# First block's output projection in rounded parts and rests, with its weights split during the attention

## The chip, the cores and the metric

The kernel runs on one core of one Trainium2 chip. The metric is the device time of one execution in microseconds (us), as the median of several runs; lower is better. The engines are TensorE (PE in the profile, with its weight loads as PEld), VectorE (DVE), ScalarE (ACT), GpSimd (POOL) and SyncE (SP), which issues the weight transfers. Each engine works through its own queue in order and waits on semaphores that other engines raise.

## The reference, cut to what matters

Two transformer blocks of two layers each run one after the other. Only the first block is touched. Each of its layers mixes tokens by two kinds of attention and a pooling, and projects the joined result back to the model width of 1024:

```python
def token_mix(qg, kg, vg, qm, km, vm, pool_in, w_pool, ls_pool, w_out):
    og = attention(qg, kg, vg, HEAD_DIM ** -0.5)       # 6 heads of 64
    om = attention(qm, km, vm, MLA_QK ** -0.5)         # 6 heads of 64
    op = multiscale_pool(pool_in, w_pool, ls_pool)     # 256 columns
    return jnp.concatenate([merge_heads(og), merge_heads(om), op], axis=-1) @ w_out
...
x_lat = x_lat + gt1 * mix
x_lat = x_lat + gt2 * sq_relu_mlp(modulate(rms_norm(x_lat, g_norm2[i]), sh2, sc2), w_mlp1[i], w_mlp2[i])
```

`w_out` is 1024 x 1024 for each layer. Layer 0 does this for 512 tokens (256 context and 256 latent tokens), layer 1 for the 256 latent tokens only. All data is float32.

## The kernel before, in words

Activations lie transposed: 128 features on the partitions, tokens along the free dimension, in 8 chunks `k` of 128 features. The mixed output is `mixT`, which is the same memory as `hT`. Its chunks 0 to 2 come from the first kind of attention, 3 to 5 from the second, 6 and 7 from the pooling. Weights come through a ring of three slots of 2 MB (`ring`), each 1024 rows by 512 columns, loaded by SP in the order of `plan_slots`; a slot is refilled when `slot_release` says that its last reader is done.

There are two ways of multiplying. The plain one uses float32 operands as they are (one instruction in the program, two matmul records in the trace). The split one cuts each operand into a part rounded to the format fp32r and the rest, also fp32r, and adds three products: high x high, high x low, low x high. MLP and second block work so. Their weights are split in **granules** of 128 output columns (8 chunks x 128 columns): ACT writes the rounded part with one copy of 128x1024 (`hi_to`, L1615), DVE the rest with one subtraction (`lo_to`, L2059), and PE's `split_product` (L1160 to L1173) waits for `lo_ready` and issues 24 matmuls. In the first block's MLP granules go through two buffers (`MLP_BUFS`), and a third one at its start. `split_by(key)` says up to which granule ACT and DVE are to split once the product `key` is done.

**Attention** (loops at L1295, L1709 and L2158). A step `j` takes 128 queries of a pair of heads: PE makes scores (L1309), DVE takes the maximum (L2165), ACT the exponential with its sum (L1736), DVE scales by the reciprocal (L2175, L2176) one step later, PE transposes the weights (L1327) two steps later, ACT copies them out of PSUM (L1726), and every second step PE multiplies by the values (L1341, bank key `"o"`) and DVE copies the result into `mixT` (L2199, L2201). Layer 0 has 24 steps, in which PE also computes modulation rows; layer 1 has 12. Two last steps compute the pooling products (L1351), which DVE copies with a gain (L2188).

**Output projection** (L1355 to L1371). It is a plain product: 8 products `m` of 128 output features, 8 chunks each, in the order 6, 7, 0 to 5. In layer 0, three small transposes of parameters (L1106) lie between the first products. As each product ends, DVE adds it with its gate to `xT` (`residual`, L2140), ACT squares the new `xT` chunk (`square_summed`, L1575) and POOL adds up the squares (L911); PE sums them over partitions (L1056, L1058), ACT takes logarithm and exponential (L1585 to L1587), DVE does one Newton step (L2042, L2044), and DVE, ACT and DVE again make the normed, shifted, rounded input of the MLP (L2083, L1625, L2068), whose first products (L1185 to L1187) follow it chunk by chunk.

The first three granules of the MLP are split by ACT after its square of chunk 2, and by DVE after its residual 5.

Of the kernel before, what the change touches and what calls it, by code (L numbers as in the profile page):

```python
# [15 lines left out]
P = 128  # L16
# [293 lines left out]

WOUT_ORDER = (6, 7, 0, 1, 2, 3, 4, 5)

# [25 lines left out]
def granules_of(i):  # L338

    g = []  # L340
    for name, _, n in mlp_slots(i):
        for m in range(4):
            key = (("a", i), "up", 4 * n + m) if name == "up" else (("a", i), "down", n % BLOCKS, n // BLOCKS * 4 + m)
            g.append(((name, i, n), m, key))
    return g


# [57 lines left out]
def program(nc, A, out):  # L405
# [5 lines left out]
    with ExitStack() as ctx:  # L411
# [65 lines left out]
        big_r = rounded_view("big", [P, 16384])  # L477
        h_hi, h_lo = hT_r, big_r[:, 2 * KC * TOK:3 * KC * TOK].rearrange("p (k t) -> p k t", k=KC)
        hid_hi, hid_lo = (big_r[:, j * KC * TOK:(j + 1) * KC * TOK].rearrange("p (k t) -> p k t", k=KC) for j in range(2))
        gran = big_r[:, 3 * KC * TOK:].rearrange("p (b a k c) -> p b a k c", b=2, a=2, k=KC)  # L480
# [60 lines left out]
        buffers = {("mlp", "third"): pair(over(3)), ("b", "h"): (hT_r[:, :, SEQ:SEQ + P], hT_r[:, :, SEQ + P:TOK]), ("b", "end"): pair(over(7)),  # L541
                   ("b", "spare"): spare, ("b", "norms"): norms, ("b", "mqk"): pair(over(4))}
        for r in range(MLP_BUFS):
            buffers["mlp", r] = (gran[:, r, 0], gran[:, r, 1])
# [35 lines left out]
        roped = sem("roped")  # L580
        pooled = sem("pooled")
        padded = sem("padded")
        nmax_ready = sem("nmax_ready")
# [109 lines left out]

        for i in range(DEPTH):
            phase(("mlp", i), granules_of(i), lambda j: ("mlp", "third" if j == 2 else (j + (j > 2)) % MLP_BUFS))
        for l in range(DEPTH):
# [30 lines left out]
        def split_by(key):  # L727

            n = gran_of[key]
            if key[0][0] == "a":  # L730
                return min(n + 1 + MLP_BUFS + (key[1] == "up" and key[2] < 2), gran_cap[n])
            return min(n + 1 + B_BUFS, gran_cap[n])
# [279 lines left out]
        def _(pe):  # L1012
# [147 lines left out]

            def split_product(n, hi, lo, T):
# [6 lines left out]
                for k in range(KC):  # L1168
                    await_chunk(k)
                    mm(b[:, 0:T], w_hi[:, k, :], hi(k), start=(k == 0), stop=False)  # L1170
                    mm(b[:, 0:T], w_hi[:, k, :], lo(k), start=False, stop=False)  # L1171
                    last = mm(b[:, 0:T], w_lo[:, k, :], hi(k), start=False, stop=(k == KC - 1))  # L1172
                fill(last, key)  # L1173
# [27 lines left out]
            for i in range(DEPTH):  # L1201
# [152 lines left out]

                for n in range(2):  # L1355
                    w = slot(("wout", i, n))
                    for m in range(4):
                        key = (tag, "wout", 4 * n + m)
                        b = start_bank(key)
                        for k in WOUT_ORDER:  # L1360
                            if n == m == 0 and k in (6, 7):
                                await_drained(pe, (tag, "pool", k - 6))
                            if n == m == 0 and k == 0:
                                await_drained(pe, (tag, "o", len(groups) - len(sets) - 1))
                            if n == m == 0 and k == 5:
                                await_drained(pe, (tag, "o", len(groups) - 1))
                            last = mm(b[:, 0:TOK - t0], w[:, k, m * P:(m + 1) * P], mixT[:, k, t0:TOK],  # L1367
                                      start=(k == WOUT_ORDER[0]), stop=(k == WOUT_ORDER[-1]))
                        fill(last, key)
                        if i == n == 0 and m > 0:  # L1370
                            params_transposed(m)  # L1371
                summed_squares((tag, "n2"), TOK - t0)
# [4 lines left out]
                for j, (name, _, _) in enumerate(mlp_slots(i)):  # L1377
                    for m in range(4):
                        n = first_gran["mlp", i] + 4 * j + m
                        if (j, m) == (0, 0):  # L1380
                            split_products_in_step(n, lambda k: h_hi[:, k, t0:TOK], lambda k: h_lo[:, k, t0:TOK], TOK - t0)
                        elif (j, m) == (0, 1):
                            if i == 0:
                                mod_column(MOD_NORM)
                        elif name == "up":
                            split_product(n, lambda k: h_hi[:, k, t0:TOK], lambda k: h_lo[:, k, t0:TOK], TOK - t0)
                        else:
                            if (4 * j + m) % 16 == 8:

                                source[0] = (up_ready, n // 16 * KC, 1)  # L1390
                            split_product(n, lambda k: hid_hi[:, k, t0:TOK], lambda k: hid_lo[:, k, t0:TOK], TOK - t0)
# [158 lines left out]
        def _(act):  # L1550
# [138 lines left out]
            for i in range(DEPTH):  # L1689
# [24 lines left out]
                steps = 2 * len(groups)  # L1714
                base = sum(24 * len(sets_of(j)) for j in range(i))
                await_drained(act, (tag, f"km{MH - 1}", 0))
                for j in range(steps + 2):
# [199 lines left out]
        def _(dve):  # L1917
# [225 lines left out]

            nm = [0]
            for i in range(DEPTH):
# [13 lines left out]
                for j in range(steps + 3):  # L2159
# [31 lines left out]
                    if 0 <= g < len(groups) and not odd:  # L2191
# [259 lines left out]
```

## Time and profile before

| what | value |
|---|---|
| median of 3 runs | 1812.45 us (1810.99 to 1812.68) |
| the profiled execution | 1810.93 us, span 1809.1 us |
| PE busy | 1747.5 us, 97% of the span |
| DVE, ACT, POOL busy | 61%, 50%, 25% |
| output projection, layer 0 | 249.7 to 305.8 us |
| output projection, layer 1 | 822.0 to 849.9 us |
| split matmuls, all lines | more than half of the chain of waits |

The span is counted from the first to the last instruction of the profiled execution; the device time also holds what lies around it. Busy shares say how long an engine had an instruction in work, not that it was at its peak.

### The profile page before, as it was taken

Reading aid. Unit: us, or ns where it says so; the run is one execution under the profiler, and the core shown is the slowest. Engines: PE = TensorE matmul, PEld = TensorE weight load, DVE = VectorE, ACT = ScalarE, POOL = GpSimd, SP = SyncE. Lnnn points to the kernel's source line nnn. Section 1 sums busy time; section 2 is a strip of 40 time slices with the busy share of each in tenths; the row PEclk is TensorE's granted clock in tenths of the full one; section 3 lists DMA queues with packets and bytes.
Section 4 is the critical chain, followed back from the end, with each engine's and each line's share of the span. In section 5 each row is a group of like instructions: output and inputs, shape, how many; then the busy total and the mean of one; then the engine's idle time right before and its main releaser. Section 6 shows DMA issues by size and latency. Waiting matters only on the chain.

```text
span 1809.1 us, 28680 instructions
## 1 busy us (share of the span) xinstructions
PE 1747.5 (97%) x10708; PEld 1424.0 (79%) x10708; DVE 1104.5 (61%) x1975; ACT 901.4 (50%) x1936; POOL 460.6 (25%) x864
## 2 busy tenths in 40 slices
PE   6999998999999998988999989999999899999998
PEld 3453553888888885647999989899899898998998
DVE  4228743887878433583555577676556686685555
ACT  3237622535353523563555566576554565674542
POOL 1017001000000010331000025057771161287730
PEclk9999999999999998999999999999999999999999
DMA  9323313455555321202445533533335335433351
GB/s 345 131 93 136 136 56 126 154 186 187 186 187 186 139 74 47 94 1 94 151 176 185 187 140 107 205 121 141 140 141 187 140 106 186 143 139 132 121 193 45
DMA packets 127540, 255.26 MB, mean 141 GB/s; under 512 B 2462, under 2 KB 7212, under 8 KB 127404
## 3 DMA queue, kind: packets, MB, share of 16 engines
q1 hardware_dynamic: 126406, 251.16, 38.8%
q0 software_dynamic: 704, 2.10, 0.4%
q8 instruction: 87, 1.43, 0.3%
q14 instruction: 49, 0.40, 0.1%
q10 hardware_dynamic: 294, 0.18, 0.0%
HBM read 252.38 MB, written 1.05 MB: 140 GB/s over the span
## 4 chain that ended last, share of the span: by engine, by line
PE 92%; DVE 4%; ACT 2%; issue 1%; DMA 0%; POOL 0%; SPq 0%; DVEq 0%; ACTq 0%
PE ps L1170 19%; PE ps L1172 18%; PE ps L1171 18%; PE ps L1195 6%; PE ps L1367 5%; PE ps L1309 2%; PE ps L1044 2%; PE ps L1428 2%; PE ps L1426 2%; PE ps L1427 2%; PE ps L1341 2%; PE ps L1327 1%; PE ps L1117 1%; PE ps L1071 1%; PE ps L1506 1%; PE ps L1509 1%
## 5 line engine op out<-in xcount | busy, mean ns | idle before, releaser
L1615 ACT ACTIVATE big_r<-ring 128x1024 fp32r<-128x1024 f32 x198 | 209.1, 1058 | 370.3 <-PE ps L1172 342.2
L2059 DVE TENSOR_TENSOR big_r<-ring,big_r 128x1024 fp32r<-128x1024 f32 x198 | 245.7, 1242 | 219.0 <-ACT big_r L1615 219.0
L1171 PE MATMUL ps<-big_r 128*128 128x256 f32 (+1 forms) x1088 | 360.6, 331 | 0.0
L1170 PE MATMUL ps<-hT_r,big_r 128*128 128x256 f32 (+1 forms) x848 | 270.6, 319 | 0.0
L1172 PE MATMUL ps<-hT_r,big_r 128*128 128x256 f32 (+1 forms) x848 | 265.6, 313 | 0.0
L911 POOL TENSOR_TENSOR sq<-sq 128x256 f32<-128x256 f32 (+1 forms) x30 | 37.1, 1238 | 741.7 <-ACT sq L1575 741.4
L1171 PEld LDWEIGHTS ps<-big_r 128*128 128x128 f32 x1088 | 206.8, 190 | 18.6
L1170 PE MATMUL ps<-big_r 128*128 128x256 f32 (+1 forms) x592 | 196.3, 332 | 1.4 <-DVE big_r L2226 1.4
L1172 PE MATMUL ps<-big_r 128*128 128x256 f32 (+1 forms) x592 | 194.8, 329 | 0.0
L1172 PEld LDWEIGHTS ps<-hT_r,big_r 128*128 128x128 f32 x848 | 161.5, 190 | 9.6
L1170 PEld LDWEIGHTS ps<-hT_r,big_r 128*128 128x128 f32 x848 | 161.6, 191 | 9.1
L2059 DVE TENSOR_TENSOR cst_r<-ring,w_ukv_sb_r 128x1024 fp32r<-128x1024 f32 x70 | 87.5, 1251 | 57.0 <-ACT w_ukv_sb_r L1615 56.9
L1170 PEld LDWEIGHTS ps<-big_r 128*128 128x128 f32 x592 | 112.5, 190 | 12.0 <-DVE big_r L2226 2.2
L1615 ACT ACTIVATE w_ukv_sb_r<-ring 128x1024 fp32r<-128x1024 f32 x70 | 74.0, 1058 | 95.6 <-PE ps L1172 83.5
L1172 PEld LDWEIGHTS ps<-big_r 128*128 128x128 f32 x592 | 112.5, 190 | 10.2
L2025 DVE SCALAR_TENSOR_TENSOR pT<-ring,csilu,pT 128x512 f32<-128x512 f32 x168 | 118.5, 747 | 1.3
L1195 PE MATMUL ps<-hT,ring 128*128 128x512 f32 (+1 forms) x288 | 107.4, 530 | 10.0 <-ACT hT L1636 9.9
L1170 PE MATMUL ps<-hT_r,w_ukv_sb_r 128*128 128x256 f32 x384 | 111.8, 291 | 0.0
L2042 DVE SCALAR_TENSOR_TENSOR nt<-ps,nt 128x256 f32<-128x256 f32 (+3 forms) x74 | 38.9, 526 | 114.9 <-ACT nt L1587 114.4
L1172 PE MATMUL ps<-hT_r,cst_r 128*128 128x256 f32 x384 | 108.2, 282 | 0.0
L1171 PE MATMUL ps<-xT_r,w_ukv_sb_r 128*128 128x256 f32 x384 | 107.7, 281 | 0.0
L1195 PEld LDWEIGHTS ps<-hT,ring 128*128 128x128 f32 x288 | 56.2, 198 | 58.9 <-issue 51.7
(317 smaller groups left out, 4332.0 us busy)
## 6 DMA issues: line engine op xcount, KB each, us to landing
ring<-in_w_in SPq DMA_DIRECT2D x44, 2048.0 KB, 7.8
ring<-in_w_mlp SPq DMA_DIRECT2D x32, 2048.0 KB, 7.7
ring<-in_w_mod SPq DMA_DIRECT2D x24, 2048.0 KB, 8.0
ring<-in_w_out SPq DMA_DIRECT2D x4, 2048.0 KB, 7.6
ring<-in_w_out_a SPq DMA_DIRECT2D x4, 2048.0 KB, 7.8
ring<-in_w_out_b SPq DMA_DIRECT2D x4, 2048.0 KB, 7.9
ring<-in_w_o SPq DMA_DIRECT2D x4, 2048.0 KB, 7.6
ring<-in_w_in SPq DMA_DIRECT2D x2, 1152.0 KB, 10.1
```

Source lines behind the costliest of these rows:

```text
L911: nc.gpsimd.tensor_tensor(sum_slot(0, T), sum_slot(0, T), sum_slot(k, T), ALU.add).then_inc(sq_summed, 1)
L1044: last = mm(b[0:parts, 0:T], ones, sq[0:parts, n % SQ, 0:T], start=(j == 0), stop=(j == chunks - 1))
L1170: mm(b[:, 0:T], w_hi[:, k, :], hi(k), start=(k == 0), stop=False)
L1171: mm(b[:, 0:T], w_hi[:, k, :], lo(k), start=False, stop=False)
L1172: last = mm(b[:, 0:T], w_lo[:, k, :], hi(k), start=False, stop=(k == KC - 1))
L1195: last = mm(b[0:cols, 0:T], w[:, k, m:m + cols], src(k), start=(k == 0), stop=(k == KC - 1))
L1309: fill(mm(banks[e][:, 0:tiles * P], lhs, rhs, start=True, stop=True), (tag, "s", 2 * j + e))
L1367: last = mm(b[:, 0:TOK - t0], w[:, k, m * P:(m + 1) * P], mixT[:, k, t0:TOK], start=(k == WOUT_ORDER[0]), stop=(k == WOUT_ORDER[-1]))
L1615: act_fn(hi, raw, ACT.Copy).then_inc(hi_ready, 1)
L2025: ins = V.scalar_tensor_tensor(acc, w, c, acc, ALU.mult, ALU.add)
L2042: drain(V.scalar_tensor_tensor(r2, bank(key)[0:parts, 0:T], width * EPS, r2, ALU.add, ALU.mult), key)
L2059: V.tensor_tensor(lo, raw, hi.bitcast(F32), ALU.subtract).then_inc(lo_ready, 1)
```

## The change

Both output projections become split products. The order of the granules is put ahead of each layer's MLP, 8 granules per layer, in three buffers laid over memory that the attention has finished with (the pooling's work area, keys and values). Granule 0 is split during the attention (ACT in step `steps - 3`, DVE in `steps - 2`), granule 1 at its end, granule 2 behind the mixed output's last chunk, and the other five as products free their buffers (`OUT_SPLIT`). The MLP's first granules are split behind residuals 5, 6 and 7.

The mixed output is split too: ACT copies each chunk rounded into `mix_hi` (over the first heads' queries, keys and values), DVE subtracts it in place. For chunks 0 to 4 this is put into the steps in `MIX_STEPS`; 6, 7 and 5 follow the last step. PE takes the chunks in `MIX_ORDER` and waits for each in the first product.

```diff
-WOUT_ORDER = (6, 7, 0, 1, 2, 3, 4, 5)
+MIX_ORDER = (0, 1, 2, 3, 4, 6, 7, 5)
+MIX_STEPS = ({16: 0, 17: 1, 18: 2, 20: 3, 24: 4}, {9: 0, 10: 1, 11: 2, 12: 3, 13: 4})
+OUT_BUFS = (0, 1, 2, 0, 1, 2, 1, 2)
+OUT_SPLIT = (4, 5, 6, 6, 7, 8, 8, 8)
...
+def granules_out(i):
+    return [(("wout", i, m // 4), m % 4, (("a", i), "wout", m)) for m in range(KC)]
...
         def split_by(key):
             n = gran_of[key]
+            if key[1] == "wout":
+                return first_gran["wout", key[0][1]] + OUT_SPLIT[key[2]]
...
 # PE
-                for n in range(2):
-                    w = slot(("wout", i, n))
-                    for m in range(4):
...
-                            last = mm(b[:, 0:TOK - t0], w[:, k, m * P:(m + 1) * P], mixT[:, k, t0:TOK],
-                                      start=(k == WOUT_ORDER[0]), stop=(k == WOUT_ORDER[-1]))
+                source[0] = (mix_ready, KC * i, 1)
+                for m in range(KC):
+                    split_product(first_gran["wout", i] + m, lambda k: mix_hi[k][:, t0:TOK], lambda k: hT_r[:, k, t0:TOK],
+                                  TOK - t0, MIX_ORDER)
...
 # ACT
+                def mix_rounded(k, made):
+                    await_drained(act, (tag,) + made)
+                    act_fn(mix_hi[k][:, t0:TOK], mixT[:, k, t0:TOK], ACT.Copy).then_inc(mix_hi_ready, 1)
...
+                    if j in MIX_STEPS[i]:
+                        k = MIX_STEPS[i][j]
+                        mix_rounded(k, ("o", made[k]))
+                    if j == steps - 3:
+                        act.wait_ge(pooled, (4, 6)[i])
+                        hi_to(o0 + 1)
+                    if j == steps:
+                        hi_to(o0 + 2)
+                for c in range(2):
+                    mix_rounded(6 + c, ("pool", c))
+                mix_rounded(5, ("o", len(groups) - 1))
+                hi_to(o0 + 3)
                 for k in range(KC):
-                    square_summed((tag, "n2"), k, (tag, "wout", k), t0)
-                    if k == 2:
-                        hi_to(first_gran["mlp", i] + MLP_BUFS + 1)
+                    key = (tag, "wout", k)
+                    await_bank(act, key)
+                    hi_to(split_by(key))
+                    square_summed((tag, "n2"), k, key, t0)
+                    if k in (5, 6):
+                        hi_to(first_gran["mlp", i] + (1 if k == 5 else MLP_BUFS + 1))
...
 # DVE
+                V.tensor_tensor(hT_r[:, k, cols], mixT[:, k, cols], mix_hi[k][:, cols].bitcast(F32), ALU.subtract)\
+                    .then_inc(mix_ready, 1)
...
+                    if j - 1 in MIX_STEPS[i]:
+                        mix_rest()
+                    if j == steps - 2:
+                        lo_to(first_gran["wout", i] + 1)
+                    if j == steps + 1:
+                        lo_to(first_gran["wout", i] + 2)
+                while n_mix[0] < KC * (i + 1):
+                    mix_rest()
...
+                lo_to(first_gran["wout", i] + 3)
                 for m in range(KC):
+                    lo_to(split_by((tag, "wout", m)))
                     residual((tag, "wout", m), m, i, 16, s0)
...
-                    if m == 5:
-                        lo_to(g0 + MLP_BUFS + 1)
+                    if m >= 5:
+                        lo_to(g0 + m - 4)
```

## Rows read from the trace of the kernel before

**Rows 1.** The page: the chain of waits, its share of the span by engine.

```profile
PE 92%; DVE 4%; ACT 2%; issue 1%; DMA 0%; POOL 0%; SPq 0%; DVEq 0%; ACTq 0%
```

**Rows 2.** Windows: stretch, us, busy us (instructions) by engine, clock, DMA share, GB/s.

```profile
249.70:305.80 56.10, 56.10 (x133) 24.74 (x133) 16.22 (x41) 7.13 (x10) 8.39 (x6) 1.00 0.10 38
```

**Rows 3.** Timeline (start us, us, engine, line): the last residual of layer 0's projection.

```profile
305.80 0.88 DVE L2140 SCALAR_TENSOR_TENSOR xT<-ps,mod,xT 128x256 f32<-128x256 f32 x2 [5.99 <-PE ps L1367]
```

**Rows 4.** Timeline, layer 1's projection: PE, a square and a split, last residual.

```profile
821.99 27.89 PE L1367 MATMUL ps<-hT,ring 128*128 128x256 f32 x128
...
833.18 0.42 ACT L1575 ACTIVATE sq<-xT 128x256 f32<-128x256 f32 x1 [3.04 <-DVE xT L2140]
833.50 1.04 ACT L1615 ACTIVATE big_r<-ring 128x1024 fp32r<-128x1024 f32 x1
...
849.93 0.48 DVE L2140 SCALAR_TENSOR_TENSOR xT<-ps,mod,xT 128x256 f32<-128x256 f32 x1 [2.10 <-PE ps L1367]
850.44 0.42 ACT L1575 ACTIVATE sq<-xT 128x256 f32<-128x256 f32 x1 [2.16 <-DVE xT L2140]
```

**Rows 5.** Timeline, MLP: successive products of 512 tokens, then of 256.

```profile
370.54 0.87 DVE L2140 SCALAR_TENSOR_TENSOR xT<-ps,mod,xT 128x256 f32<-128x256 f32 x2
375.99 0.87 DVE L2140 SCALAR_TENSOR_TENSOR xT<-ps,mod,xT 128x256 f32<-128x256 f32 x2
...
905.03 1.06 ACT L1615 ACTIVATE big_r<-ring 128x1024 fp32r<-128x1024 f32 x1 [1.82 <-PE ps L1172]
906.12 1.23 DVE L2059 TENSOR_TENSOR big_r<-ring,big_r 128x1024 fp32r<-128x1024 f32 x1 [1.26 <-ACT big_r L1615]
907.26 0.48 DVE L2140 SCALAR_TENSOR_TENSOR xT<-ps,mod,xT 128x256 f32<-128x256 f32 x1
907.91 1.06 ACT L1615 ACTIVATE big_r<-ring 128x1024 fp32r<-128x1024 f32 x1 [1.82 <-PE ps L1172]
```

**Rows 6.** Timeline, MLP: rounding and rest of 512 tokens, rest of 256.

```profile
329.87 0.63 ACT L1768 ACTIVATE big_r<-sq 128x512 fp32r<-128x512 f32 x1
334.40 0.68 DVE L2226 TENSOR_TENSOR big_r<-sq,big_r 128x512 fp32r<-128x512 f32 x1
...
866.01 0.42 DVE L2226 TENSOR_TENSOR big_r<-sq,big_r 128x256 fp32r<-128x256 f32 x1
```

**Rows 7.** Timeline, end of layer 0's attention, idle time before in brackets.

```profile
240.43 0.69 DVE L2165 TENSOR_REDUCE stat<-ps 128x1 f32<-128x512 f32 x1 [0.62 <-PE ps L1309]
...
242.72 1.22 PE L1327 MATMUL ps<-cst,pb 128*128 128x128 f32 x8 [0.24 <-DVE pb L2176]
...
246.55 0.60 ACT L1726 ACTIVATE rstd<-ps 128x512 f32<-128x512 f32 x1 [1.97 <-PE ps L1327]
```

**Rows 8.** Timeline, end of layer 1's attention.

```profile
812.34 0.69 DVE L2165 TENSOR_REDUCE stat<-ps 128x1 f32<-128x512 f32 x1 [0.62 <-PE ps L1309]
...
813.97 1.09 ACT L1726 ACTIVATE pT<-ps 128x512 f32<-128x512 f32 x2 [2.52 <-PE ps L1327]
...
814.62 1.22 PE L1327 MATMUL ps<-cst,pb 128*128 128x128 f32 x8 [0.59 <-ACT pT L1726]
```

**Rows 9.** Timeline, layer 1: splits of DVE beside sums of POOL.

```profile
843.42 4.01 DVE L2059 TENSOR_TENSOR big_r<-ring,big_r 128x1024 fp32r<-128x1024 f32 x3
...
844.03 1.19 POOL L911 TENSOR_TENSOR sq<-sq 128x256 f32<-128x256 f32 x1 [2.73 <-ACT sq L1575]
...
848.36 0.72 POOL L911 TENSOR_TENSOR sq<-sq 128x256 f32<-128x256 f32 x1 [3.14 <-ACT sq L1575]
```

**Rows 10.** The window behind layer 1's projection, and two matmuls in it.

```profile
855.00:861.00 6.00, 5.28 (x25) 5.31 (x26) 5.70 (x13) 3.28 (x8) 0.00 (x0) 0.51 0.34 123
...
855.72 0.55 PE L1185 MATMUL ps<-hT_r,big_r 128*128 128x256 f32 x1 [4.11 <-DVE big_r L2068]
...
856.29 0.41 PE L1187 MATMUL ps<-hT_r,big_r 128*128 128x256 f32 x1
856.50 0.41 PE L1185 MATMUL ps<-hT_r,big_r 128*128 128x256 f32 x1
```

More of the change, by code:

```diff
@@ L478, in program @@
         h_hi, h_lo = hT_r, big_r[:, 2 * KC * TOK:3 * KC * TOK].rearrange("p (k t) -> p k t", k=KC)
+        mix_hi = [big_r[:, o:o + TOK] for o in [k * TOK for k in range(5)] + [4608 + k * TOK for k in range(3)]]
         hid_hi, hid_lo = (big_r[:, j * KC * TOK:(j + 1) * KC * TOK].rearrange("p (k t) -> p k t", k=KC) for j in range(2))
@@ L542, in program @@
                    ("b", "spare"): spare, ("b", "norms"): norms, ("b", "mqk"): pair(over(4))}
+        for r, o in enumerate((13376, 8192, 10240)):
+            v = big_r[:, o:o + 2 * KC * P].rearrange("p (a k c) -> p a k c", a=2, k=KC)
+            buffers["out", r] = (v[:, 0], v[:, 1])
         for r in range(MLP_BUFS):
@@ L581, in program @@
         pooled = sem("pooled")
+        mix_hi_ready = sem("mix_hi_ready")
+        mix_ready = sem("mix_ready")
         padded = sem("padded")
@@ L694, in program @@
         for i in range(DEPTH):
+            phase(("wout", i), granules_out(i), lambda j: ("out", OUT_BUFS[j]))
             phase(("mlp", i), granules_of(i), lambda j: ("mlp", "third" if j == 2 else (j + (j > 2)) % MLP_BUFS))
@@ L1159, in await_chunk, with split_product @@
                         source[0] = None
-            def split_product(n, hi, lo, T):
+            def split_product(n, hi, lo, T, order=tuple(range(KC))):
                 key = granules[n][2]
@@ L1167, in split_product @@
                 w_hi, w_lo = gran_bufs[n]
-                for k in range(KC):
-                    await_chunk(k)
-                    mm(b[:, 0:T], w_hi[:, k, :], hi(k), start=(k == 0), stop=False)
+                for j, k in enumerate(order):
+                    await_chunk(j)
+                    mm(b[:, 0:T], w_hi[:, k, :], hi(k), start=(j == 0), stop=False)
                     mm(b[:, 0:T], w_hi[:, k, :], lo(k), start=False, stop=False)
-                    last = mm(b[:, 0:T], w_lo[:, k, :], hi(k), start=False, stop=(k == KC - 1))
+                    last = mm(b[:, 0:T], w_lo[:, k, :], hi(k), start=False, stop=(j == KC - 1))
                 fill(last, key)
@@ L1353, in _ @@
                         fill(last, key)
-                for n in range(2):
-                    w = slot(("wout", i, n))
-                    for m in range(4):
[L1358 to L1366, printed above, removed]
-                            last = mm(b[:, 0:TOK - t0], w[:, k, m * P:(m + 1) * P], mixT[:, k, t0:TOK],
-                                      start=(k == WOUT_ORDER[0]), stop=(k == WOUT_ORDER[-1]))
-                        fill(last, key)
-                        if i == n == 0 and m > 0:
-                            params_transposed(m)
+                source[0] = (mix_ready, KC * i, 1)
+                for m in range(KC):
+                    split_product(first_gran["wout", i] + m, lambda k: mix_hi[k][:, t0:TOK], lambda k: hT_r[:, k, t0:TOK],
+                                  TOK - t0, MIX_ORDER)
+                    if i == 0 and 0 < m < 4:
+                        params_transposed(m)
                 summed_squares((tag, "n2"), TOK - t0)
@@ L1388, in _ @@
                             if (4 * j + m) % 16 == 8:
-                                source[0] = (up_ready, n // 16 * KC, 1)
+                                source[0] = (up_ready, (i * BLOCKS + j // 4) * KC, 1)
                             split_product(n, lambda k: hid_hi[:, k, t0:TOK], lambda k: hid_lo[:, k, t0:TOK], TOK - t0)
@@ L1715, in _ @@
                 base = sum(24 * len(sets_of(j)) for j in range(i))
+                o0 = first_gran["wout", i]
+                def mix_rounded(k, made):
+                    await_drained(act, (tag,) + made)
+                    act_fn(mix_hi[k][:, t0:TOK], mixT[:, k, t0:TOK], ACT.Copy).then_inc(mix_hi_ready, 1)
+                half, n_sets = len(groups) // 2, len(sets)
+                made = [half - 1] * 3 + [half + n_sets - 1, half + 2 * n_sets - 1]
                 await_drained(act, (tag, f"km{MH - 1}", 0))
@@ L2142, in residual, with mix_rest @@
                 drain(last, key)
-            nm = [0]
+            n_mix = [0]
+            def mix_rest():
+                i, k = n_mix[0] // KC, MIX_ORDER[n_mix[0] % KC]
+                n_mix[0] += 1
+                dve.wait_ge(mix_hi_ready, n_mix[0])
+                cols = slice(t0_of(i), TOK)
+                V.tensor_tensor(hT_r[:, k, cols], mixT[:, k, cols], mix_hi[k][:, cols].bitcast(F32), ALU.subtract)\
+                    .then_inc(mix_ready, 1)
             for i in range(DEPTH):
```

## Prediction

> **What bounds the kernel now.** I read the chain of waits first: PE has 92% of it [rows 1], so the time is the sum of PE's work and the few places where PE waits. The window of layer 0's projection then shows PE busy in 56.10 of 56.10 us at full clock, DVE in 16.2, ACT in 7.1, DMA at 0.10 [rows 2]: this stage costs what its matmuls cost, and both engines that the change loads have room. The timelines give its ends: from the window's start to the last residual at 305.80 in layer 0, 56.1 us [rows 2, 3]; 821.99 to 849.93 in layer 1, 27.9 us [rows 4]. Last come the ends of the attentions, where small work is put between steps: DVE sat idle only 0.62 us before a maximum, and PE already waits there, 0.24 us for DVE in layer 0 and 0.59 us for ACT in layer 1 [rows 7, 8].
>
> **Part 1, PE in layer 0.** Removed: 8 plain products in 56.1 us, of which three small transposes take about 0.6, so 6.94 each. Added: 8 split products of 24 matmuls at 512 tokens. The MLP makes exactly these; two residuals behind successive ones start 5.45 us apart [rows 5]. 8 x 5.45 + 0.6 = 44.2. Gain 11.9 us, if PE is fed.
>
> Is it fed? A granule after product m costs in a row: ACT's rounding, then DVE's rest 1.09 later, DVE's residual 1.14 behind that [rows 5] and lasting 0.88, ACT's square about 0.65 (as the 0.63 rounding of the same width [rows 6]). That is 3.8 us against 5.45 for a product, and each granule is wanted two products after its buffer is free (one product later for the last two). The parameters' copies and scalings come behind products 1 to 3 on DVE, whose 16.2 us with them leave room for 8 rests of 1.23 in 44 [rows 2]. At the end: product 5 ends at t; split of granule 7, residual and square to t+3.8; first MLP granule's rest done at t+6.2; residual 6 to t+7.1, square to t+7.8, next rounding and rest to t+10.1. Product 7 ends at t+10.9 and finds DVE free. Nothing lost in layer 0.
>
> **Part 2, PE in layer 1.** The same products at 256 tokens take 2.88 us (granule roundings at 905.03 and 907.91 [rows 5]), 8 x 2.88 = 23.0 instead of 27.9. By PE alone 4.9 less. But here the row of ACT and DVE is longer than the product. ACT's square to its next rounding 0.32 (833.18 to 833.50 [rows 4]), rounding to rest 1.09, rest to residual 1.14 [rows 5], residual to square 0.51 (849.93 to 850.44 [rows 4]): 3.06 us per link, and the order of the code forces it: ACT rounds granule n+1 only behind its square n, which waits for residual n, which DVE does only behind rest n. With S the start of product 0: product 4 ends at S+14.4, by when product 3, which splits nothing, has let the engines catch up. Then rounding of granule 6, its rest and residual 4 at S+14.4+0.05+1.09+1.14 = S+16.7. Three links follow (granule 7 with residual 5, MLP granule 0 with residual 6, MLP granule 1 with residual 7): residual 7 at S+16.7+9.2 = S+25.9, though its product is done at S+23.0. Granule 6 is ready at S+16.7 and wanted at S+17.3, granule 7 at S+19.8 and wanted at S+20.2, so PE itself waits little; only the tail is late. Against S+27.9 before [rows 4] the gain is 2.0, not 4.9.
>
> **Part 3, work put into the attentions.** Per layer DVE gets 5 rests of chunks and 2 of granules, ACT 5 roundings of chunks and 2 of granules, before the last step ends. In layer 0 a chunk is 0.63 on ACT and 0.68 on DVE [rows 6], a granule 1.06 and 1.23. ACT waited 1.97 us for PE before its copies of the last step [rows 7], longer than chunk 4 or granule 1 alone, and somewhat like it in the steps before; it takes them in. DVE does too with single chunks. The rest of granule 0 however (step 22) lies before a maximum with 0.62 us of idle time, and PE's transposes behind it already waited 0.24 for DVE [rows 7]: 1.23 - 0.62 = 0.6 us on the path. Bounds: 0, and everything on DVE, 5 x 0.68 + 2 x 1.23 = 5.9. I take 0.6, by the nearest row.
>
> In layer 1 step 10 has a chunk (0.42 [rows 6]) and granule 0 together, 1.65 us before a maximum with 0.62 idle, so 1.0 later on DVE; PE's transposes begin at 814.62 and end 1.2 us later, a part of the delay falls on their second half, and what reaches the values' product I put at 0.8. ACT's own 1.5 us in step 9 vanish in 2.52 us of waiting two steps on [rows 8]. Bounds 0 and 5 x 0.42 + 2 x 1.23 = 4.6; I take 0.8.
>
> **Part 4, the new wait of product 0.** It waits chunk by chunk for `mix_ready`. Behind it on PE are all further products, on the others nothing before the first residual. The last attention result is copied by DVE (0.42), then in layer 1 four rests (chunks 4, 6, 7, 5) of 0.42 on DVE, with ACT's rounding of 5 (0.42, as its square of this width [rows 4]) beside them: ready 2.2 us after PE's last value product. PE comes to chunk 5, the eighth, after 7/8 of 2.88 = 2.5. In layer 0 it is 0.42 + 3 x 0.68 = 2.5 against 4.8. Price 0; if the cover goes, as much as DVE is late, at most some 1.5 us (granule 1's rest plus a handover) in layer 1.
>
> **Part 5, behind the projection.** After residual 7 one more MLP rest (1.23) is on DVE. Beside it run ACT's square and three functions of 0.42 each before DVE is wanted, 1.7 us without PE's sums: hidden. Slots are released earlier, when granules 3 and 7 are split; DMA has nothing to do there (share 0.10 [rows 2]). PE idles longer in layer 1, from S+23.0. Behind the idle 4.11 us the clock was granted at 0.51 in 855 to 861, matmuls 0.21 us apart [rows 10] instead of 2.88/24 = 0.12: that is the 1.2 GHz level. After the change the fall may come before the last sum of squares; two float32 records of 256 tokens more slowly, 0.3 us. Bounds -1 (it rises sooner) and +2.
>
> What DVE and POOL do to each other speaks against the change. Three rests took 4.01 us instead of 3.7, and the POOL sum beside them 1.19 instead of 0.72 [rows 9]. In the new order a sum of 256 tokens runs during ACT's rounding (1.09 until DVE starts) and is out of the way, so I put nothing into the sum. The Trainium skill, GPSIMD Engine Reference, Specifications, says that GpSimd shares its SBUF interfaces with VectorE, with contention against instructions that have two SBUF inputs, as the rests do. The trace agrees by those numbers. By that rule alone each of six rests in layer 1 that met a sum would be 0.1 us longer, 0.6 us in all.
>
> **Sum.** Layer 0: -11.9 + 0.6. Layer 1: -2.0 + 0.8. Behind: +0.3. Together -12.2 us. The profiled execution took 1810.93 (span 1809.1, 1.8 outside it) and would take 1798.7. It lies 1.5 us below the median 1812.45; I apply the difference to the median: 1800.2.
>
> **Rivals.**
> - *Layer 1 follows PE.* If ACT and DVE run ahead of the order above, residual 7 comes at S+23.0: 2.9 more, -15.1, 1797.3. For it: DVE was busy in 16.2 of 56.1 us of such a stage [rows 2]. Against: the links are fixed by the queues' order. 0.12.
> - *The attentions pay for all of it.* DVE's added work comes fully onto the path, 5.9 + 4.6 instead of 1.4: +9.1, so -3.1, 1809.3. For: PE waits for DVE and ACT there already. Against: ACT's idle times of 1.97 and 2.52 us [rows 7, 8]. Halfway, 1804.8, is likelier than the whole. Together 0.13, of which the full case 0.07.
> - *Granules come late.* PE in layer 1 is held by each link, 8 x 3.06, and in layer 0 by the buffers, one link of 3.8 us lost: -8, 1804. Against: buffers are three. 0.07.
> - *Slower: the clock falls in the projection.* The waits for chunks in product 0 and the late tail let it fall to the lower level and stay there. At 0.21 us per matmul of 256 tokens [rows 10] and twice that at 512, a product takes 5.1 and 10.3 us. 8 x (10.3 - 5.45) + 8 x (5.1 - 2.88) = 57 us more than in the forecast, so 1857. It decides once about a fifth of the matmuls (12.2 of 57) run so. Against: it stood at 1.00 through the whole plain stage [rows 2], and the MLP's split products kept their pace at full clock [rows 5]. 0.03.
> - *It does not do what it says*: a wait of granule 0 for pooling or weights moves the splitting behind the attention; each layer then starts some 3 us late, 1806. Against: the slots were asked for long before, DMA was at 0.10 when the stage began [rows 2]. 0.03.
>
> **How the numbers follow.** The forecast has 0.62, with 1797.5 to 1803 as its own range. With the others, 8 in 10 lie within 1796.5 to 1805.5. Within 0.2% of 1812.45, about what can be told from no change, is 1808.8 to 1816.1: the full attention case, 0.07. Slower 0.03, faster 0.90.
>
> **What would show it.** The new profile should have split matmuls 0.227 us apart in layer 0 and a stage of 44 to 45 us; in layer 1, residual 7 about 26 us after the stage begins with PE idle nearly 3 us before it, and residuals in its last third 3.1 us apart, not 2.9. The values' product of the last group should come 0.6 and 0.8 us later after the attention's start. I am wrong if layer 1's stage takes 23 us, if PE waits over 1 us inside product 0, or if the first projection starts over 2 us late.

## The result, and the profile after

The changed kernel takes 1797.98 us, the median of 5 runs (1795.74 to 1801.34), beside 1810.99 for the kernel before in the same rounds: a ratio of 0.993, with an interval of 0.9913 to 0.9948. It is 13.0 us faster (9 to 16); 1800.2 and -12.2 were forecast. The profiled execution is the one of 1797.98, so its trace can stand for the median.

The page of the changed kernel, its first part:

```profile
span 1796.1 us, 29026 instructions
PE 1731.1 (96%) x10836; PEld 1433.7 (80%) x10836; DVE 1127.6 (63%) x2007; ACT 924.6 (51%) x1968; POOL 459.8 (26%) x864
```

DVE and ACT have each gained some 23 us of work, PE has lost 16, and the span is 13.0 us shorter: it went with PE, not with the helpers. Windows of the changed kernel, with the columns of [rows 2]: layer 0's projection, then layer 1's tail:

```profile
250.10:295.00 44.90, 44.90 (x198) 36.51 (x197) 22.77 (x49) 14.43 (x18) 7.74 (x6) 1.00 0.26 94
833.00:843.00 10.00, 3.44 (x17) 2.14 (x16) 6.10 (x9) 4.57 (x10) 0.73 (x1) 0.72 0.54 202
```

The first row answers to [rows 2]: PE is again busy in all of it at full clock, the stage is just shorter. The second shows where layer 1 is not PE's. Timeline of the changed kernel, layer 0: the end of the attention, the first split matmuls, the last residual:

```profile
240.08 1.22 DVE L2091 TENSOR_TENSOR big_r<-ring,big_r 128x1024 fp32r<-128x1024 f32 x1
241.21 1.28 DVE L2206 TENSOR_REDUCE stat<-ps 128x1 f32<-128x512 f32 x2
243.23 1.22 PE L1346 MATMUL ps<-cst,pb 128*128 128x128 f32 x8 [0.40 <-DVE pb L2217]
...
250.17 0.50 PE L1189 MATMUL ps<-big_r 128*128 128x512 f32 x1
...
254.17 0.39 PE L1191 MATMUL ps<-big_r 128*128 128x512 f32 x1
254.40 0.39 PE L1189 MATMUL ps<-big_r 128*128 128x512 f32 x1
254.62 0.39 PE L1190 MATMUL ps<-hT_r,big_r 128*128 128x512 f32 x1
...
295.02 0.88 DVE L2172 SCALAR_TENSOR_TENSOR xT<-ps,mod,xT 128x256 f32<-128x256 f32 x2 [0.62 <-PE ps L1191]
```

The rest of granule 0 now stands before the maximum, and PE's wait for DVE behind it is 0.40 us where it was 0.24 [rows 7]. The matmuls start 0.23 us apart. From the first of them to the last residual it is 44.85 us; it was 56.1 [rows 2, 3].

Timeline of the changed kernel, layer 1: a wait in the attention, and the last three links of the row of ACT and DVE, with PE's sums of squares:

```profile
803.78 1.22 PE L1346 MATMUL ps<-cst,pb 128*128 128x128 f32 x8 [1.08 <-DVE pb L2217]
...
831.21 0.48 DVE L2172 SCALAR_TENSOR_TENSOR xT<-ps,mod,xT 128x256 f32<-128x256 f32 x1
831.72 0.42 ACT L1583 ACTIVATE sq<-xT 128x256 f32<-128x256 f32 x1 [1.69 <-DVE xT L2172]
832.04 1.04 ACT L1623 ACTIVATE big_r<-ring 128x1024 fp32r<-128x1024 f32 x1
833.12 1.23 DVE L2091 TENSOR_TENSOR big_r<-ring,big_r 128x1024 fp32r<-128x1024 f32 x1 [1.44 <-ACT big_r L1623]
834.26 0.48 DVE L2172 SCALAR_TENSOR_TENSOR xT<-ps,mod,xT 128x256 f32<-128x256 f32 x1
...
836.19 0.67 PE L1075 MATMUL ps<-sq,cst 128*128 128x256 f32 x2 [1.65 <-POOL sq L930]
...
837.36 0.48 DVE L2172 SCALAR_TENSOR_TENSOR xT<-ps,mod,xT 128x256 f32<-128x256 f32 x1
...
838.39 1.22 PE L1077 MATMUL ps<-sq,cst 128*128 128x256 f32 x2 [1.53 <-ACT sq L1583]
```

Residuals start at 831.21, 834.26 and 837.36: 3.05 and 3.10 us apart, against the 2.88 of a product. PE is done at about 834.5 and waits 1.65 us, then 1.53 us more. The stage begins at 811.15, so residual 7 comes 26.21 us behind it, where it was 27.94 [rows 4].

| us | before | after | difference | forecast |
|---|---|---|---|---|
| layer 0: first scores to projection | 84.67 | 84.83 | +0.16 | +0.6 |
| layer 0: projection to last residual | 56.14 | 44.85 | -11.3 | -11.9 |
| layer 1: first scores to projection | 45.37 | 45.86 | +0.49 | +0.8 |
| layer 1: projection to last residual | 27.94 | 26.21 | -1.7 | -2.0 |
| layer 1: last residual to first Newton step | 3.12 | 3.69 | +0.57 | +0.3 |
| sum | | | -11.8 | -12.2 |

Of the other 1.2 us, 0.57 lie behind that Newton step: to the first matmul of the MLP's third product, the first that does not go chunk by chunk behind the normed input, it was 10.78 us and is 10.21. The others are pieces of 0.4 to 0.6 us, with either sign, elsewhere in code that is not changed. Between two profiles an untouched stretch can differ by more. Layer 1's attention is the same code in x1_residual_first below, and took 47.32 us there instead of 45.86. A window at its start, in that run, has the reason:

```profile
763.60:766.90 3.30, 3.30 (x8) 1.47 (x10) 0.80 (x3) 0.00 (x0) 3.14 (x5) 0.50 0.00 0
```

The clock was granted at 0.50 there, up to 766.9; in the changed kernel it was 1.00 in this stretch. From the first scores to the first ones of the second kind of attention it is 16.92 us in x1 and 15.46 in the changed kernel, which is the whole difference of 1.46. For the pieces of 0.4 to 0.6 I give no cause.

### The profile page after: what moved, and what is told of

It reads as the page before. It is cut to its first block, busy times and chain, and to the rows that moved or that the text cites. A ratio compares the mean times of both kernels' runs of the same rounds, so it can differ in the third digit from the quotient of the medians.

```text
span 1796.1 us, 29026 instructions
## 1 busy us (share of the span) xinstructions
PE 1731.1 (96%) x10836; PEld 1433.7 (80%) x10836; DVE 1127.6 (63%) x2007; ACT 924.6 (51%) x1968; POOL 459.8 (26%) x864
## 4 chain that ended last, share of the span: by engine, by line
PE 51%; DVE 1%; ACT 1%; issue 0%; POOL 0%; DVEq 0%; ACTq 0%
PE ps L1189 12%; PE ps L1191 12%; PE ps L1190 12%; PE ps L1436 2%; PE ps L1434 2%; PE ps L1435 2%; PE ps L1514 1%; PE ps L1517 1%; PE ps L1509 1%; PE ps L1090 1%; PE ps L1063 1%; PE ps L1480 1%; PE ps L1204 0%; PE ps L1205 0%; ACT big_r L1623 0%; DVE big_r L2091 0%
## 5 line engine op out<-in xcount | busy, mean ns | idle before, releaser
L2091 DVE TENSOR_TENSOR big_r<-ring,big_r 128x1024 fp32r<-128x1024 f32 x214 | 263.9, 1233 | 249.3 <-ACT big_r L1623 249.2
L1623 ACT ACTIVATE big_r<-ring 128x1024 fp32r<-128x1024 f32 x214 | 226.2, 1058 | 370.8 <-PE ps L1191 358.3
L1190 PE MATMUL ps<-big_r 128*128 128x256 f32 (+1 forms) x1088 | 360.6, 331 | 0.0
L1189 PE MATMUL ps<-big_r 128*128 128x256 f32 (+1 forms) x720 | 239.9, 333 | 1.4 <-DVE big_r L2277 1.4
L1191 PE MATMUL ps<-big_r 128*128 128x256 f32 (+1 forms) x720 | 237.9, 330 | 0.0
L1190 PEld LDWEIGHTS ps<-big_r 128*128 128x128 f32 x1088 | 206.8, 190 | 18.7
L1189 PEld LDWEIGHTS ps<-big_r 128*128 128x128 f32 x720 | 136.8, 190 | 15.2 <-DVE big_r L2277 2.2
L1191 PEld LDWEIGHTS ps<-big_r 128*128 128x128 f32 x720 | 136.8, 190 | 12.8
```

Source lines behind the costliest of these rows:

```text
L1189: mm(b[:, 0:T], w_hi[:, k, :], hi(k), start=(j == 0), stop=False)
L1623: act_fn(hi, raw, ACT.Copy).then_inc(hi_ready, 1)
L2091: V.tensor_tensor(lo, raw, hi.bitcast(F32), ALU.subtract).then_inc(lo_ready, 1)
```

## The experiments

My theory was that of the forecast: layer 0 follows PE; layer 1 follows the order rounding, rest, residual, square; granule 0's rest is the price in the attentions; the chunks cost nothing. The rival in layer 1 was that PE or contention bounds it, and in the attentions that each added split has its share of the price. Effects under 1 us are read from stages in the profiles, since times of one kernel spread over 2 to 6 us. All edits are to the changed kernel.

**x1_residual_first.** DVE does the residual ahead of the next rest.

```diff
 for m in range(KC):
-    lo_to(split_by((tag, "wout", m)))
     residual((tag, "wout", m), m, i, 16, s0)
+    lo_to(split_by((tag, "wout", m)))
```

> On VectorE each residual of the projection goes ahead of the rest of the next granule instead of behind it; all else is the changed kernel. Theory (layer 1's stage is set by the order rounding, rest, residual, square, 3.06 us a link): with the residual first a granule is ready 2.3 us after its buffer is free and the square does not wait for it, so links vanish among the projection's own granules; the MLP's granules still stand before residuals 6 and 7. Residual 7 of layer 1 starts 24.2 us after the stage begins instead of 26.2, layer 0 unchanged (44.9 us). Rival (the order is harmless, PE or the clock holds layer 1): 26.2 stays.

Measured: 1796.77 (one run; before 1810.64). Layer 1's stage is 24.67 us (811.90 to 836.57), layer 0's 44.86 as before the edit. The same instructions in another order give 1.5 us: it is the order, not DVE's load. The last three residuals still have a rest between them that only the MLP wants. The stage is 0.5 us longer than expected, and 0.4 of that is one rest. Timeline of this kernel, layer 1, DVE and POOL:

```profile
830.64 2.90 DVE L2091 TENSOR_TENSOR big_r<-ring,big_r 128x1024 fp32r<-128x1024 f32 x2 [0.69 <-ACT big_r L1623]
831.00 1.47 POOL L930 TENSOR_TENSOR sq<-sq 128x256 f32<-128x256 f32 x1 [1.41 <-ACT sq L1583]
...
833.47 0.47 DVE L2172 SCALAR_TENSOR_TENSOR xT<-ps,mod,xT 128x256 f32<-128x256 f32 x1
```

The second of the two rests started beside the sum and took 1.65 us instead of 1.23, and residual 6 came right behind it.

**x2_tail_free.** As x1, and the rests of the first MLP granules moved behind their residuals:

```diff
-                    if m >= 5:
-                        lo_to(g0 + m - 4)
+                    if m == KC - 2:
+                        lo_to(g0 + 1)
+                lo_to(g0 + MLP_BUFS + 1)
```

> As the kernel before it, and also the rests of the MLP's first granules are moved on VectorE: the first behind residual 6, the other two behind residual 7. Theory: residual 7 of layer 1 starts when its product is done, 23.1 us after the stage begins (26.2 in the changed kernel), so 3.0 us less in all; two rests of 1.23 us fit ahead of the Newton step. Layer 0 unchanged. The clock may fall later too: 0 to 0.6 us more. Rival (the Newton step becomes late because two rests lie before it): 1 us is given back. Total 1795 if the theory holds, 1798 if not.

Measured: 1793.47 (1792.75 to 1794.96, 4 runs; ratio to before 0.9913, 0.9897 to 0.993). Timeline of this kernel, layer 1, DVE, and PE's first matmul of the stage:

```profile
809.32 0.39 PE L1189 MATMUL ps<-big_r 128*128 128x256 f32 x1
...
826.90 0.49 DVE L2172 SCALAR_TENSOR_TENSOR xT<-ps,mod,xT 128x256 f32<-128x256 f32 x1 [0.48 <-PE ps L1191]
828.07 1.23 DVE L2091 TENSOR_TENSOR big_r<-ring,big_r 128x1024 fp32r<-128x1024 f32 x1 [0.69 <-ACT big_r L1623]
829.78 0.48 DVE L2172 SCALAR_TENSOR_TENSOR xT<-ps,mod,xT 128x256 f32<-128x256 f32 x1 [0.48 <-PE ps L1191]
830.18 1.21 DVE L2091 TENSOR_TENSOR big_r<-ring,big_r 128x1024 fp32r<-128x1024 f32 x1
832.65 0.48 DVE L2172 SCALAR_TENSOR_TENSOR xT<-ps,mod,xT 128x256 f32<-128x256 f32 x1 [1.26 <-PE ps L1191]
```

Each residual now waits for PE, in brackets, where in the changed kernel it came straight behind a rest. They are 2.88 and 2.87 us apart, and the stage is 23.33 us: 8 x 2.88 and the last residual's handover. Now layer 1 follows PE, and the 2.9 us between the forecast and its first rival are what the order had cost in this stage. (In time the medians differ by 4.5 us; 0.5 more lie between residual 7 and the Newton step, see part 5 below, and the rest is within what the times spread.)

**x3_granule0_later.** Granule 0's rest goes behind the last step's maximum and scaling, in both layers (`j == steps - 2` becomes `j == steps`).

> On VectorE the rest of projection granule 0 goes from step steps-2 to step steps, where no maximum follows. Theory (granule 0 ahead of a maximum costs 0.5 us in each attention): PE waits no more 0.4 us in layer 0 and 1.1 us in layer 1 for the scaled weights, and both projections begin about 0.5 us earlier in their attentions. Rival (single chunks cost it, or another wait stands right behind): the starts do not move.

Measured: 1796.55 (one run). Timeline of this kernel in layer 0:

```profile
240.31 0.69 DVE L2206 TENSOR_REDUCE stat<-ps 128x1 f32<-128x512 f32 x1 [0.62 <-PE ps L1328]
...
242.60 1.22 PE L1346 MATMUL ps<-cst,pb 128*128 128x128 f32 x8 [0.24 <-DVE pb L2217]
...
245.29 1.22 DVE L2091 TENSOR_TENSOR big_r<-ring,big_r 128x1024 fp32r<-128x1024 f32 x1
```

The idle 0.62 before the maximum and PE's wait of 0.24 are those of [rows 7] again, with the rest behind them. Layer 1's attention takes 45.37, the number of before. The other profiles bear this out: from the first scores of the second kind to the projection, layer 1 takes 30.40 or 30.41 us wherever this rest stands ahead of the maximum (the changed kernel, x1, x2, x4, x6, x10) and 29.91 where it does not (before, x3, x7, x8, x9); in layer 0 it is likewise 48.93 or 48.94 with it and 48.77 or 48.78 without. So all of the price was this rest, and the other splits had none, but in layer 0 it was 0.16 us and not the 0.5 that I expected here too.

**x5_no_spread.** The five first chunks are split behind the attention and not in its steps: `MIX_STEPS = ({}, {})`, and ACT rounds chunks 0 to 4 ahead of the pooled ones.

> The changed kernel with no chunk of the mixed output split inside the attention: chunks 0 to 4 are rounded and subtracted behind the last step, ahead of 6, 7 and 5. Theory (single chunks inside the steps cost nothing, so taking them out wins nothing; what they save is a wait in product 0): the way from the ninth attention result to the last one is as in the changed kernel, and product 0 waits for its first chunk (copy 0.4, rounding 0.3 to 0.6, rest 0.4 to 0.7 us) and then nearly keeps pace, so 1 to 2 us more in each layer before product 0 ends. Rival (the chunks in the steps are what delays the attentions): the projections start earlier by 0.2 and 0.5 us.

Measured: 1798.85 (one run). From layer 0's copy of the sixth last group (the first of the second kind) to that of the last it takes 31.86 us, with the chunks inside the steps 31.87: in there they were free. Timeline of this kernel at the start of the projections, DVE's last copy, its rests, and PE's first split matmul in layers 0 and 1:

```profile
250.96 0.42 DVE L2244 COPY hT<-ps 128x256 f32<-128x256 f32 x1 [1.17 <-PE ps L1360]
251.30 3.09 DVE L2185 TENSOR_TENSOR hT_r<-hT,big_r 128x512 fp32r<-128x512 f32 x5
...
252.13 0.47 PE L1189 MATMUL ps<-big_r 128*128 128x512 f32 x1 [1.21 <-DVE hT_r L2185]
...
812.70 0.35 PE L1189 MATMUL ps<-big_r 128*128 128x256 f32 x1 [0.94 <-DVE hT_r L2185]
```

Product 0 waits 1.21 us for chunk 0 and then keeps its pace, as the chunks come faster than PE's three matmuls each. From the last copy's start to residual 7 it is 45.96 us instead of 44.74 in layer 0, 27.08 instead of 26.10 in layer 1. So spreading them is worth 1.2 and 1.0 us.

**x9_layer0_only, x6_layer1_only.** The change in one layer, the plain projection of before with its granules' slots in the other; each product, granule split and chunk split is put under `if i == ONLY`.

> The split projection in layer 0 alone, the plain one in layer 1. Theory (the gains of the layers add, nearly all is layer 0's): stage of layer 0 44.9 us, of layer 1 27.9 us; 11 us less than before, 1799.5 by a median of 1810.7. Rival (part of the gain comes only with both): under 9 less.

> The split projection in layer 1 alone; layer 0 has the plain one of the kernel before. Theory (layer 1 wins 1.7 in its stage and pays 0.5 before it, 0 to 0.6 us of clock behind it): 1.2 us less than before, 1809.5 by a median of 1810.6; stage of layer 0 56.1 us, of layer 1 26.2 us. Rival (layer 1 follows PE): 4.4 less.

Measured: layer 0 alone 1798.35 (1798.16 to 1801.21, 4 runs; before 1810.77; ratio 0.9936, 0.9919 to 0.9953), its stage 44.84 us and the plain one of layer 1 27.93. Layer 1 alone 1809.82 (1807.77 to 1811.47, 10 runs; before 1810.73; ratio 0.9996, 0.9987 to 1.0006), its stage 26.23. The layers add up: -12.4 and -0.9 beside -13.0. Layer 1's part can't be told from nothing in time; only its profile shows it: 1.7 gained in the stage and 0.5 paid back ahead of it. The 0.57 us that the changed kernel paid behind it are not there: from the last residual to the Newton step it is 3.17 us, against 3.12 before.

**x4_two_terms.** The products of the projections leave out the matmul of the weights' rests, so the output is less exact; PE has 16 of 24 matmuls, ACT and DVE all their work.

```diff
-                    last = mm(b[:, 0:T], w_lo[:, k, :], hi(k), ...)
+                    if not two:
+                        last = mm(b[:, 0:T], w_lo[:, k, :], hi(k), ...)
```

> The projection leaves out its third term, the rest of the weights times the rounded mixed output; the rests are still made. 16 instead of 24 matmuls per product. Theory: layer 0 is PE's, 5.45 us a product, and becomes 3.63 us by PE, then is held by the link of ScalarE and VectorE at 512 tokens, about 3.7 us plus the parameters' work: residual 7 at about 33 instead of 44.9 us after the stage begins. Layer 1 is the engines' order already: 26.2 becomes 25.5 to 26.2 though a third of its matmuls is gone. Rival (PE holds both): layer 1 becomes 15.4 us + tail, under 21.

Measured: 1784.75 (one run). Timeline of this kernel, residuals of layer 1, whose first split matmul starts at 800.91:

```profile
815.43 0.47 DVE L2173 SCALAR_TENSOR_TENSOR xT<-ps,mod,xT 128x256 f32<-128x256 f32 x1
818.48 0.48 DVE L2173 SCALAR_TENSOR_TENSOR xT<-ps,mod,xT 128x256 f32<-128x256 f32 x1
821.53 0.48 DVE L2173 SCALAR_TENSOR_TENSOR xT<-ps,mod,xT 128x256 f32<-128x256 f32 x1
824.63 0.48 DVE L2173 SCALAR_TENSOR_TENSOR xT<-ps,mod,xT 128x256 f32<-128x256 f32 x1
```

And PE's first matmul of product 5:

```profile
812.03 0.36 PE L1189 MATMUL ps<-big_r 128*128 128x256 f32 x1 [0.91 <-DVE big_r L2092]
```

With a third of PE's work gone they are still 3.05, 3.05 and 3.10 us apart: the link of 3.06 sets the pace, not PE. The stage is 23.72, though, and I had expected 25.5 to 26.2. That was my error: I let the row of links start where product 4 of full length ends, with residual 4 at S+16.7. Here residual 4 comes at S+14.5. That is not PE's doing either, as product 4 was done at S+10: residuals 0, 1 and 2 are already 3.05 us apart (they start at 805.70, 808.75 and 811.80), and PE waits for granules 5, 6 and 7. With short products the links hold the whole stage, and PE with it. Layer 0 is 33.6 us.

**x10_two_terms_tail_free.** x4 with the order of x2; the same is left out.

> The free tail with the third term of the projection left out (16 matmuls per product, the rest of the weights unused). Theory (the order rounding, rest, residual, square held layer 1, and the free tail has taken it away): with two thirds of the matmuls layer 1's stage shrinks by nearly a third of PE's 23, to 16 to 18 us, where with the old order the same cut stopped at 23.7. A granule is ready 2.3 us after its buffer is free and a product now takes 1.9, so the last two may wait 0.5 each. Rival (something else of the order, the buffers or POOL's sums, is behind 23): it stays over 20.

Measured: 1774.11 (one run). Timeline of this kernel, layer 1:

```profile
796.57 0.38 PE L1189 MATMUL ps<-big_r 128*128 128x256 f32 x1
...
811.44 0.49 DVE L2173 SCALAR_TENSOR_TENSOR xT<-ps,mod,xT 128x256 f32<-128x256 f32 x1 [0.42 <-PE ps L1190]
813.34 0.48 DVE L2173 SCALAR_TENSOR_TENSOR xT<-ps,mod,xT 128x256 f32<-128x256 f32 x1 [0.28 <-PE ps L1190]
```

Layer 1's stage is 16.77 us, 6.95 less than with the same instructions in the order of the changed kernel, and layer 0's is 30.35 instead of 33.6. With short products the order costs in both layers.

**x7_tail_and_granule0.** x2 and x3 together.

> The changed kernel with three moves on VectorE: residuals ahead of the next granule's rest, the MLP's first rests behind residuals 6 and 7, projection granule 0 in step steps. Theory (the two findings are independent): layer 1's stage 23.3 us, both attentions 0.2 and 0.5 us shorter than in the changed kernel; 0.7 less than with the free tail alone, 1792.8. Rival (they overlap): as with the free tail alone, 1793.5.

Measured: 1794.14 (1793.04 to 1795.14, 4 runs; ratio 0.991, 0.9895 to 0.9924). The stages are those expected: attention 45.37 and projection 23.33 in layer 1. The time is not below that of x2; 0.7 us are less than these runs can tell.

**x8_clock_held.** x7, with four matmuls whose result nobody reads between layer 1's sum of squares and its MLP:

```diff
                 summed_squares((tag, "n2"), TOK - t0)
+                if i == 1:
+                    for _ in range(4):
+                        mm(ps[:, 7, :], cc("ones"), cst[:, 0:512], start=True, stop=True)
```

> The kernel before it, and in layer 1 four float32 matmuls of 512 columns into an unused bank between the last sum of squares and the MLP, where PE idles 4.1 us; their result is not used. Theory (that idle time lets the clock fall to the lower level, and the MLP's first matmuls pay): with PE kept at work they run 0.12 us apart from the start, and from the Newton step to the third product of the MLP it takes 9.3 us instead of 10.2; 0.9 less in all. Rival (the clock falls anyway, or VectorE and ScalarE set the pace there): 10.2 stays, and the added matmuls run at half rate and delay the MLP by up to 1 us.

Measured: 1793.26 (1791.9 to 1795.01, 4 runs; ratio 0.9904, 0.9887 to 0.992). The window at the start of the MLP, x7 and then x8:

```profile
836.00:842.00 6.00, 3.57 (x17) 3.60 (x18) 5.51 (x14) 2.85 (x6) 0.00 (x0) 0.50 0.06 21
```

```profile
836.00:842.00 6.00, 5.32 (x23) 3.10 (x22) 5.15 (x12) 2.97 (x7) 0.00 (x0) 1.00 0.31 113
```

And PE's first MLP matmul and the next but two in x8:

```profile
839.81 0.35 PE L1204 MATMUL ps<-hT_r,big_r 128*128 128x256 f32 x1 [0.68 <-DVE big_r L2106]
...
840.24 0.28 PE L1204 MATMUL ps<-hT_r,big_r 128*128 128x256 f32 x1
840.35 0.28 PE L1205 MATMUL ps<-big_r 128*128 128x256 f32 x1
```

In x7 PE idles 4.12 us there and then runs at a granted clock of 0.50, the 1.2 GHz level; in x8 the clock stays at 1.00 and matmuls are 0.12 us apart, not 0.21. From the Newton step to the MLP's third product it is 9.61 us instead of 10.41. But among the profiles of the changed kernel and its variants, which all have the same code there, only x10's is as long: it is 9.80 us in x6, 9.85 in x1, 9.99 in x3 and 10.21 in x2 and in the changed kernel. So the lower clock costs something here, as forecast, and holding it up is worth 0.8 us against this one profile and 0.2 us against the best. In the times no gain can be told: 0.9 us between the medians, with runs that spread over 2 to 3.

x2, x7 and x8 beat both kernels, by 16.6 to 17.5 us against before and about 4 against the change; among the three the times don't decide.

## Why the prediction was right

The time lies 2.2 us under the forecast and in its own range, 0.5 us above its lower end, and the likeliest case is the one that happened. Of the 2.2 us, 1.5 are the kernel before, whose median was 1812.45 for the forecast and is 1810.99 now. That the parts sum to -11.8 where -12.2 was forecast is in part luck: the two stages and the tail were 0.6, 0.3 and 0.3 too good, and the price in the attentions, 0.75 too high, made up for most of it.

*Part 1, layer 0.* Right in kind, 0.6 us too good. PE was busy throughout, no granule was late. The stage is 44.85 and not 44.2: 8 x 5.44 are 43.5, and the three transposes break the pace by 0.14, 0.39 and 0.45 us (I had 0.6 for all). The other 0.35 are at the two ends: 0.15 in product 0, whose second matmul starts 0.33 us behind the first where others start 0.23 apart, and 0.2 from the end of the last product's pace to residual 7. x9 has the same 44.84.

*Part 2, layer 1.* Right: 26.2 against 25.9, with links of 3.05 to 3.10 where 3.06 was worked out, and PE idle for 3.2 us before the last sum. The 0.3 us over is the start of the row: ACT's rounding of granule 6 began at 825.92, 0.28 us behind the first matmul of product 5 (825.64), where I had put 0.05. x1, x2, x4 and x10 show that it is the order of the queues. The rival by which layer 1 follows PE (23.0) came true only when the order was changed (23.3). That one link's length can be had from four starts in a timeline of before is the part of the working that held best.

*Part 3, the attentions.* The place was right, one rest of 1.22 us before a maximum, and x3 shows that nothing else cost. The size was not: 0.16 and 0.49 for 0.6 and 0.8. I took the rest less the idle time before the maximum as the delay. But DVE does two maxima there. In x3 they take 0.69 each with 0.17 us idle between them, 1.55 from the first's start to the second's end; behind the rest, with both inputs there, they run together in 1.28. So 0.43 us of delay at the first are 0.16 at the end. What reaches PE is 0.40 - 0.24 = 0.16 in layer 0, and 1.08 for DVE in place of 0.59 for ACT, 0.49 more, in layer 1. The rival in which the attentions pay for all of it is out: 0.65 in place of 10.5.

*Part 4.* Right: in the changed kernel product 0 shows no wait, and x5, which takes the cover away, pays 1.2 and 1.0 us.

*Part 5.* Right in kind, 0.57 for 0.3: the last float32 pair took 1.22 us at the lower clock. But this size is that of one profile, and the code of the tail does not fix it. x3, x5 and x6 have the same instructions in this tail; there the clock was still at 1.00 when the pair ran. Timeline of x3, PE, and a window of it just behind:

```profile
837.86 0.70 PE L1077 MATMUL ps<-sq,cst 128*128 128x256 f32 x2 [1.53 <-ACT sq L1583]
...
839.30:846.00 6.70, 3.33 (x15) 3.37 (x16) 5.55 (x13) 3.24 (x8) 0.00 (x0) 0.50 0.01 2
```

PE had waited the same 1.53 us as in the changed kernel, yet the clock fell only behind the pair. From the last residual to the Newton step it is 3.17, 3.18 and 3.17 us in these three, against 3.69 in the changed kernel and 3.12 before. To the MLP's third product it is 13.16, 13.27 and 12.97 us, and 13.90 both before and in the changed kernel. So nothing of this term was left in the changed kernel's profile, and in the three others the tail was 0.6 to 0.9 us shorter than before. That the two cancelled in the changed kernel is luck: my working had nothing on where in this tail the clock falls.

*DVE and POOL.* In layer 1 no rest grew: all eight in the stage took 1.22 or 1.23 us, since the sums ran during ACT's rounding (832.22 for 0.74, rest at 833.12), as the order said. In layer 0 two did. Timeline of the changed kernel:

```profile
288.07 1.30 POOL L930 TENSOR_TENSOR sq<-sq 128x512 f32<-128x512 f32 x1 [4.09 <-ACT sq L1583]
288.98 1.47 DVE L2091 TENSOR_TENSOR big_r<-ring,big_r 128x1024 fp32r<-128x1024 f32 x1 [1.65 <-ACT big_r L1623]
```

A sum of 512 tokens is longer, overlaps the rest by 0.4 us, and the rest takes 1.47 instead of 1.23. DVE still waited 0.62 us for PE before the last residual, so the stage did not pay for it. The Trainium skill, GPSIMD Engine Reference, Specifications, has the two share their SBUF interfaces, with contention against instructions that have two SBUF inputs. The trace agrees where they meet, with 0.24 us; in layer 1 they never met, so the 0.6 us that the rule alone would have given did not arise.

They do meet in layer 1 once the residual goes first. Timeline of x2_tail_free, POOL, beside the rest of 828.07 shown above:

```profile
828.42 1.47 POOL L930 TENSOR_TENSOR sq<-sq 128x256 f32<-128x256 f32 x1 [1.41 <-ACT sq L1583]
```

Four of the six sums in this stage took 1.47 us like this one instead of 0.74, while the rest that had started 0.35 us before it kept its 1.23. In x1 and in layer 0 of the changed kernel it is the rest that started second, and the rest that is longer. In all these rows the one that starts second pays.

The other side, a falling clock in the projection, did not come near: 1.00 in all of layer 0's stage.

**What stays open:** the 0.6 us and less by which other unchanged stretches differ between the two profiles, what decides where in layer 1's tail the clock falls, and whether x8's gain is there in time and not only in its profile.

## What to carry to other kernels

Moving work from the bounding engine to idle ones gives what that engine loses only where the product is longer than the row of handovers that the queues' order makes of the helpers' work: write down one link, from square to square, and compare it with the product, for each size of tile. Where the link is longer, put what others wait for (the residual) ahead of what is wanted later (the rest), and keep work for the next stage out of the tail: here that was worth 2.9 us in layer 1's stage, where splitting itself had brought 1.7. A split that goes into steps with idle time was free here, if it stands behind the instruction that the bounding engine waits for and not ahead of it.

## What the runs showed of the hardware

- Handovers between ACT and DVE were small: the rest starts 0.04 us behind the end of its rounding (832.04 + 1.04 to 833.12), the square 0.03 to 0.08 us behind its residual (831.21 + 0.48 to 831.72, 834.26 + 0.48 to 834.82). On one engine the next instruction starts 0.1 us before the recorded end of the one before it (the rounding at 832.04, the square until 832.14). So a link of 3.05 us is nearly the sum of its four instructions, 3.17.
- After 4.1 us of idle time PE ran at 0.50 of the clock at the start of the MLP. Four matmuls with no use kept it at 1.00 (x8), for 0.2 to 0.8 us less to the MLP's third product than in the profiles without them.
- Two float32 records of 256 tokens took 0.67 us at full clock and 1.22 at the lower one, in one and the same kernel 2.2 us apart. The later pair, behind the same idle time of 1.53 us, took 0.70 in x3: one tail can meet the lower clock in one profile and miss it in another.
- A rest of DVE and a sum of POOL that overlap: the one that starts second is longer, the other is not. A sum of 256 tokens behind the start of a rest took 1.47 us instead of 0.74 (x2), a rest behind the start of a sum of 512 tokens 1.47 instead of 1.23 (changed kernel), and behind that of a sum of 256 tokens 1.65 (x1).
